# Sparse-attention scores as three single-pass products of split queries and keys instead of one fp32 product

## The reference

```python
qh = q.reshape(...) * (HEAD_DIM ** -0.5)          # 6 heads of 64, in 2 key/value groups of 3
s_s = jnp.einsum('bkgqd,bkqjld->bkgqjl', qi, k_sel).astype(f32) - sl[..., None] * dist[:, :, None]
p_s, _ = _softmax_masked(...)
s_w = jnp.einsum('bkgqd,bknd->bkgqn', qi, kwi).astype(f32) - sl * rel.astype(f32)
p_w, _ = _softmax_masked(s_w, m_w)
o = gi[..., 0:1] * o_c + gi[..., 1:2] * o_s + gi[..., 2:3] * o_w
```

## Time and profile before

| what | value |
|---|---|
| median of 3 runs | 725.65 us (725.53 to 728.75) |
| the profiled execution | 728.8 us |
| its span, first to last instruction | 727.0 us |
| PE busy | 706.1 us (97%) |
| PEld busy | 568.8 us (78%) |
| DVE busy | 450.1 us (62%) |
| ACT busy | 365.3 us (50%) |
| mean granted TensorE clock | 0.992 |

### The profile page before, as it was taken

How to read it: one execution, slowest core, us unless ns; L and a number is a source line. 1 busy time by engine, 2 the same in 40 slices (tenths; PEclk the granted TensorE clock), 3 DMA queues, 4 the chain that set the end, 5 groups by cost and what they waited for, 6 DMA issues and landing times. The chain is left out here.

```text
span 727.0 us, 10208 instructions
## 1 busy us (share of the span) xinstructions
PE 706.1 (97%) x4182; PEld 568.8 (78%) x4182; DVE 450.1 (62%) x647; ACT 365.3 (50%) x565; POOL 11.6 (2%) x20
## 2 busy tenths in 40 slices
PE   5999999999999999999999999999999999999898
PEld 5889888889755566887887888778887888887787
DVE  2677873347655555266369748694659759649544
ACT  6673554565565654347545444443445343264641
POOL 2000000000000000003000000000000000000000
PEclk9999999999999999999999999999999999999899
DMA  9505333320210103731213251134112123313102
GB/s 357 206 36 174 121 138 115 110 91 35 86 60 5 54 2 117 283 151 53 72 50 117 71 218 59 58 116 174 58 59 103 71 87 115 117 59 115 59 14 102
DMA packets 13838, 74.31 MB, mean 102 GB/s; under 512 B 1824, under 2 KB 3904, under 8 KB 6112
## 3 DMA queue, kind: packets, MB, share of 16 engines
q1 hardware_dynamic: 13392, 70.56, 27.1%
q0 software_dynamic: 256, 3.11, 1.0%
q10 hardware_dynamic: 144, 0.00, 0.0%
HBM read 70.51 MB, written 2.10 MB: 100 GB/s over the span
## 5 line engine op out<-in xcount | busy, mean ns | idle before, releaser
L1636 PE MATMUL bank<-Xhi,Whi 128*128 128x512 f32 (+1 forms) x480 | 188.3, 392 | 2.2 <-DVE Wlo L1446 1.0
L1637 PE MATMUL bank<-Xlo,Whi 128*128 128x512 f32 (+1 forms) x480 | 186.2, 388 | 0.0
L1638 PE MATMUL bank<-Xhi,Wlo 128*128 128x512 f32 (+1 forms) x480 | 186.2, 388 | 0.0
L1636 PE MATMUL bank<-Whi,Uhi 128*128 128x512 f32 (+1 forms) x304 | 116.7, 384 | 0.8 <-DVE Wlo L1101 0.5
L1637 PE MATMUL bank<-Wlo,Uhi 128*128 128x512 f32 (+1 forms) x304 | 114.9, 378 | 0.0
L1638 PE MATMUL bank<-Whi,Ulo 128*128 128x512 f32 (+1 forms) x304 | 114.9, 378 | 0.0
L1636 PEld LDWEIGHTS bank<-Xhi,Whi 128*128 128x128 f32 x480 | 90.7, 189 | 26.9 <-issue 6.9
L1638 PEld LDWEIGHTS bank<-Xhi,Wlo 128*128 128x128 f32 x480 | 90.7, 189 | 18.6
L1637 PEld LDWEIGHTS bank<-Xlo,Whi 128*128 128x128 f32 x480 | 90.8, 189 | 17.3
L1101 DVE TENSOR_TENSOR Wlo<-raw,Whi 128x2048 fp32r<-128x2048 f32 x28 | 64.1, 2290 | 48.7 <-ACT Whi L713 48.7
L1110 DVE TENSOR_TENSOR Wlo<-arena,Whi 128x2048 fp32r<-128x2048 f32 x20 | 45.7, 2287 | 51.1 <-ACT Whi L721 51.1
(11 more groups left out here) (230 smaller groups left out, 867.0 us busy)
## 6 DMA issues: line engine op xcount, KB each, us to landing
raw<-wst SPq DMA_DIRECT2D x43, 1024.0 KB, 4.8
arena<-wst SPq DMA_DIRECT2D x16, 1024.0 KB, 4.9
arena<-ctab POOLq DMA_DIRECT2D x1, 2880.0 KB, 9.6
arena<-xn SPq DMA_DIRECT2D x4, 512.0 KB, 5.1
arena<-xn SPq DMA_DIRECT2D x1, 2048.0 KB, 7.6
out<-arena SPq DMA_DIRECT2D x7, 256.0 KB, 2.0
arena<-gpost SPq DMA_DIRECT2D x2, 512.0 KB, 7.2
arena<-arena SPq DMA_DIRECT2D x8, 64.0 KB, 2.0
```

What stands on the lines that cost most here:

```text
L1636: mm(out_ap, w[0], x[0], start=start, stop=False, **kw)
L1637: mm(out_ap, w[0], x[1], start=False, stop=False, **kw)
L1638: return mm(out_ap, w[1], x[0], start=False, stop=stop, **kw)
```

## The change

The scores of the 24 units are made from halves. The queries and keys are split ahead: `PARTS` lists five tiles (KS, Q0, KW, Q0+1, Q0+2) and the slot of `Uhi` and `Ulo` that each goes to. ScalarE makes the high halves (`part_high`) and VectorE the low halves (`part_low`): the first two ahead of unit 0, the others in units 0, 1 and 2. `scores` waits for the halves it reads and issues three products for each k, the two k side by side. Since slots 3 and 4 now hold keys, the recurrence's output is kept in a new place `OH` and split at u=21 and u=24. To make room for `OH`, the transposed weights `PT` are packed as triangles.

```diff
-        PT = view(aX, 8192).rearrange("p (a k j t) -> p a k j t", a=2, k=NKV, j=TT)
+        PTW = 13 * P
+        OH = view(aX + 7168, 1024)
+        def pt_columns(a, k, i):
+            o = aX + (NKV * a + k) * PTW + i * P
+            return view(o, 384 * (i + 1)).rearrange("p (j n) -> p j n", n=384)[:, :, 0:P]
+        def pt_rows(a, k, j):
+            return view(aX + (NKV * a + k) * PTW + 4 * j * P, (TT - j) * P)
...
+        PARTS = ((3, KS), (0, Q0), (4, KW), (1, Q0 + 1), (2, Q0 + 2))
+        PART_AT = {0: 2, 1: 3, 2: 4}
...
+                    def part_high(n):
+                        place, tile = PARTS[n]
+                        nc.scalar.activation(Uhi[:, place, :], T[:, tile, :], ACT.Copy).then_inc(qk_hi, 1)
+                    act.wait_ge(job_done, H_JOB[1] + 1)
+                    act.wait_ge(ct_lo, 1)
+                    part_high(0)
+                    part_high(1)
...
-                        if u == 3:
-                            for j in range(2):
-                                act.wait_ge(oh_done, 1)
-                                nc.scalar.activation(Uhi[:, 3 + j, :], tD[:, j * SEQ:(j + 1) * SEQ],
-                                                     ACT.Copy).then_inc(mix_hi, 1)
+                        if u in PART_AT:
+                            part_high(PART_AT[u])
+                        if u in (21, NU):
+                            j = (21, NU).index(u)
+                            act.wait_ge(oh_done, 1)
+                            act.wait_ge(s_mm, NKV * (20 if j == 0 else NU))
+                            nc.scalar.activation(Uhi[:, 3 + j, :], OH[:, j * SEQ:(j + 1) * SEQ],
+                                                 ACT.Copy).then_inc(mix_hi, 1)
...
+                    def part_low(n):
+                        place, tile = PARTS[n]
+                        dve.wait_ge(qk_hi, n + 1)
+                        V2.tensor_tensor(Ulo[:, place, :], T[:, tile, :], Uhi[:, place, :].bitcast(fp32),
+                                         ALU.subtract).then_inc(qk_lo, 1)
+                    part_low(0)
+                    part_low(1)
...
-                        if u == 4:
-                            hg_lo()
+                        if u in PART_AT:
+                            part_low(PART_AT[u])
+                        if u in (21, NU):
+                            hg_lo((21, NU).index(u))
...
-                        for k in range(NKV):
-                            r = slice(k * HD, (k + 1) * HD)
-                            mm(PB[2 * (u % 2) + k][:, 0:(i + 1) * P], T[r, Q0 + g, i * P:(i + 1) * P],
-                               T[r, (KS, KW)[b], 0:(i + 1) * P], start=True, stop=True).then_inc(s_mm, 1)
+                        pe.wait_ge(qk_lo, max(2 if b == 0 else 3, (2, 4, 5)[g]))
+                        for n, (q, kv) in enumerate(((Uhi, Uhi), (Uhi, Ulo), (Ulo, Uhi))):
+                            for k in range(NKV):
+                                r = slice(k * HD, (k + 1) * HD)
+                                last = mm(PB[2 * (u % 2) + k][:, 0:(i + 1) * P], q[r, g, i * P:(i + 1) * P],
+                                          kv[r, 3 + b, 0:(i + 1) * P], start=(n == 0), stop=(n == 2))
+                                if n == 2:
+                                    last.then_inc(s_mm, 1)
```

More of the change, by code:

```diff
@@ L161, in build @@
         SQ, RS = tA.rearrange("p (j t) -> p j t", j=2), tC.rearrange("p (j t) -> p j t", j=2)
[L163 removed]
+        PTW = 13 * P
+        OH = view(aX + 7168, 1024)
+        assert 2 * NKV * PTW <= 7168
+        def pt_columns(a, k, i):
[3 more added lines that the diff above has]
+            return view(aX + (NKV * a + k) * PTW + 4 * j * P, (TT - j) * P)
         SR = view(aX + 8192, SRD * NKV * SEQ).rearrange("p (a n) -> p a n", a=SRD * NKV)
@@ L301, in build @@
         oh_done = sem("oh_done")
+        qk_hi = sem("qk_hi")
+        qk_lo = sem("qk_lo")
         mix_hi = sem("mix_hi")
@@ L864, in t_copy @@
                             act.wait_ge(t_mm, NKV * u + k + 1)
-                            nc.scalar.activation(PT[:, a, k, 0:i + 1, i * P:(i + 1) * P],
+                            nc.scalar.activation(pt_columns(a, k, i),
                                                  PB[TRB[k]][:, 0:(i + 1) * P].rearrange("p (j t) -> p j t", t=P),
@@ L1304, in hg_out, with hg_lo @@
                         dve.wait_ge(hgo_ev, 2)
[L1305 to L1311, removed]
+                        V2.tensor_tensor(OH, tB, tC, ALU.mult).then_inc(oh_done, 1)
+                    def hg_lo(j):
+                        dve.wait_ge(mix_hi, (2, 4)[j])
+                        V2.tensor_tensor(Ulo[:, 3 + j, :], OH[:, j * SEQ:(j + 1) * SEQ], Uhi[:, 3 + j, :].bitcast(fp32),
+                                         ALU.subtract).then_inc(mix_lo, 1)
+                    def part_low(n):
[5 more added lines that the diff above has]
+                    part_low(1)
                     def cmp_keys():
@@ L1428, in _ @@
                             if grp in (1, 3) and part == TT - 1:
-                                mix_lo_part(grp // 2, 2 + grp // 2 + 1)
+                                mix_lo_part(grp // 2, grp)
                     dve.wait_ge(mix_hi, 6)
@@ L1954, in values @@
                             pe.wait_ge(t_ev, NKV * TT * (grp + 1))
-                            if b == 0:
-                                pe.wait_ge(mix_lo, 2 + g)
+                            if b == 0 and g:
+                                pe.wait_ge(mix_lo, g if g == 1 else 3)
                         for k in range(NKV):
                             last = mm(PB[OB][k * HD:(k + 1) * HD, s * P:SEQ], V[:, (VS, VW)[b], s, k * HD:(k + 1) * HD],
-                                      PT[:, grp % 2, k, s, s * P:SEQ], start=(b == 0 and s == 0), stop=False)
+                                      pt_rows(grp % 2, k, s), start=(b == 0 and s == 0), stop=False)
                         if b == 1 and s == TT - 1:
```

## The result

The changed kernel took **728.89 us** (median of 18 runs, 727.65 to 730.97), the kernel before 725.73 us (18 runs, 722.89 to 728.87). The medians are 3.2 us apart; the ratio is 1.0039, 95% interval 1.0025 to 1.0053, which is 0.4% slower or some 2.8 us. The forecast was 728.1 us and 2.5 us more. The profiled execution of the changed kernel took 730.89 us, with a span of 728.2 us against 727.0 before.

A forecast was written before the change was run, and what follows sets the result against it. TensorE, busy 97% of the span, was taken as the bound. Pause 2.7 plus split 0.5 less 0.7 kept from the scores gave 2.5 us more: 725.65 becomes 728.1 us, range 723.5 to 733.5.

The forecast's parts named there:

- of it lost in waits: Scores blocks ahead of waits set by ScalarE and VectorE: net 0.26 us of the gain disappears into longer waits.
- rival C: The 2.7 us pause ahead of unit 0 makes the clock fall: 1.5 us more, 729.6 us; chance 0.20.
- Step 1: 24 scores blocks: three overlapping pairs of half-type products, fixed 0.21 us kept; 1.0 us less, 0.7 of it kept.
- Step 2: Ahead of unit 0's scores: TensorE idles 2.7 us for one ScalarE copy, then two VectorE subtractions.
- Step 3: Other splits: `part_high(2)` ahead of panel 15's split makes the wait at 162.44 grow by 0.5 us.
- The parts costed at nothing: Parts 3 and 4 in units 1 and 2: late rows of units 2 and 3 are covered, no cost.
- At u=24: Output split: rows of unit 25 start 0.75 us late, at most 0.2 comes through, costed at nothing.
- A: Scores blocks: pairs of half-type products do not overlap, six distances paid; 13.8 us more, 739.5 us; chance 0.10.
- B: Scores blocks: second and third weight loads of the same rows wait for the matmul ahead; 5.3 more, 733.4 us; chance 0.07.
- D: 128-key scores blocks: products cost the upper bound, 0.21 us each; 1.6 more, 729.2 us; chance 0.15.
- E: Scores blocks: the fixed 0.21 us belongs to float32 and vanishes; 5.0 less, about 723.5 us; chance 0.07.

The follow-up runs named there:

- e1: Changed kernel with TensorE's spread matmuls of unit 0, and ScalarE's copies to match, put ahead of unit 0's scores: 724.14 us, ratio 0.9986.
- e2: Kernel before, float32 scores, with the same reordering as e1 (spread of unit 0 ahead of its scores): 725.39 us, ratio 1.0011.
- e7: Changed kernel with a fourth product, low x low, in each of the 24 units: one run, 731.76 us beside 726.02.
- e8: e1 with VectorE's low halves of the later panels moved one unit later, behind that unit's rows and scaling: 720.54 us, ratio 0.9943.
- e9: Kernel before, float32 scores, with both reorderings of e8: 721.37 us, ratio 0.9949.
- e3: Changed kernel with all its splits and waits, but scores again made as one float32 matmul per half: 729.40 us, ratio 1.0059.
- e6: Changed kernel with ten unused 512-column matmuls keeping TensorE busy in the pause ahead of unit 0, scores no earlier: 727.81 us, ratio 1.0029.
- e4: Changed kernel with the loops exchanged, the three products of one k issued first, then the three of the other: 728.85 us, ratio 1.0051.
- e5: Changed kernel with the selected keys (KS) split earlier, so one low half instead of two stands ahead of unit 0: 727.75 us, ratio 1.0035.

## Why the prediction was right

728.1 us was forecast and 728.89 measured, within 0.5% of the kernel before. By its steps:

| term | forecast | measured |
|---|---|---|
| pause ahead of unit 0 | +2.7 | +2.78 |
| split of panel 15 later | +0.5 | +0.52 |
| blocks, all 24 | -1.0 | -1.8 (e1 against e2) |
| of it lost in waits | 0.26 | 0.6 |
| clock | 0 (rival C: +1.5) | +2.8 for one fall, -1.5 for another, in the two profiles |
| stage | +2.5 | +3.43 |

**Step 1** had its mechanism right: fixed part kept, three distances, pairs side by side. 0.89, 0.72 and 0.545 us are the forecast's 0.90, 0.735 and 0.57. The mis-sized term is the 128-key block: I took 0.12 for each distance and left the fixed 0.21 beside it, and got 0.57; it is 0.48. e7 shows why: its inner steps are 0.11, the distance of the weight loads and the lower bound I had, and the first step of 0.16 already holds part of the fixed 0.21. Six such blocks are 0.5 of the 0.8 us by which the gross gain was underrated. **What is lost in waits** grew with the gain, and ends just where it was said to: behind units 2, 7, 11 and 18, by 0.07, 0.21, 0.22 and 0.08. The kept gain is 1.2 (e1 against e2) instead of 0.7. e8 and e9 bear the cause out, since without these waits all of it arrives.

**Step 2** came out to 0.1 us, with its whole chain. **Step 3** too: 0.83 in e3 against 0.31 before. (Half of 1.16 is 0.58, which the forecast put down as 0.5; 0.52 came.) The parts costed at nothing brought no wait between unit 2's and unit 7's. At u=24 the low half ran at 265.65 and the rows of unit 25 began at 267.31, 2.36 later than in the earlier trace rows; some 1.9 of it is the shift of the whole stage, so 0.5 is left of the 0.75 allowed for. A new wait of 0.09 at 256.24 and 0.10 more at 280.81 are all that TensorE shows from unit 21 on.

**The rivals.** A, B, D and E are refuted by the blocks and the loads above: 0.89 us, neither 1.59 nor 0.7, and 0.48 at 128 keys. B was a rule of the Trainium skill, TensorE: Matmul & The Clock Gate, Part 3 (the mechanism), by which a load overlaps matmuls in flight only when its row group differs. The trace disagrees in every block: the load at 213.70 goes to the rows on which the product of 213.59 is running, and the next product starts only at 213.93. The same section also lets a load run ahead when it goes to the background weight buffer, and with that the trace is consistent.

**C came true**, at a chance of 0.20: the forecast itself had the clock at nothing. C had its part as one more fall of 1.5 us. In the profiled execution the fall after the pause took 2.8 (0.68 on the first block, 2.1 on the spread and `cmp_mlp` behind it; e6, without it, is 2.9 shorter), about twice, since it was 6.8 us long; and the old fall after unit 3, worth 1.5, was gone, though the 24 small products stand there as before. The net +1.3, less the 0.5 us more that was kept of the blocks, carries the forecast's 2.5 nearly to the 3.43 of the stage. The old fall is absent from the one profile of all ten other kernels, e2 and e9 with their float32 products among them, and in e2, e6 and e8, at 0.998, the only fall ahead of the span's end stands between 668 and 674 us. The 31 of 46 executions of before at 0.998 have room for one such fall, so most of them probably lack the one in the stage. The prediction read it in an execution that it knew to be 3.1 us above the median, and took it for a trait of the kernel. Why it comes in some executions and not in others stays open.

For the medians this gives a simpler account. Without the clock the change costs 2.78 + 0.52 - 1.2 = 2.1 us, and the executions at 0.998 are 2.2 apart. The median execution went from 0.998 to 0.995, and the medians are 3.2 apart, which leaves 1.1 for the clock. So the forecast was 0.4 too high in what it summed, since it kept too little of the blocks' gain, and lacked 1.1 for the clock. That the two misses have opposite signs is luck, and it brought 728.1 as near to 728.89 as it is; the costs of the pause and of the split are not.

## What to carry to other kernels

A new operand form has two prices, and the second is where it is made: with TensorE busy for 97% of the span, the two copies and two subtractions ahead of the first use cost 2.8 us of idle, and the fall of the clock behind it as much again in the profiled execution (1.1 by the medians), while the cheaper scores gave back 1.2. Put work that doesn't need the new operand there (e1 turned 0.4% slower into 0.1% faster). Then look at which waits lie behind the places that got faster: a third of the gain went into them, and moving the work that ends them (0.4% from e1 to e8, 0.6% from e2 to e9) was worth more than the change itself. And before a fall of the clock is read out of a profile, compare that execution's time and mean clock with the others': here both main profiles had a lower mean clock than their medians.

## What was not expected of the hardware

- The order of two independent 64-row streams in the program hardly matters (0.16 us over 24 blocks): e4 issues three products of one half of the rows and then three of the other, and the trace has the same pairs at the same times to 0.01 us (213.59, 213.93, 214.16). The Trainium skill, TensorEngine Tiling (Array Packing), Key Properties, says that tiles can load and multiply independently of each other; the trace agrees, and shows it for the order of issue too.
- A pair of half-type products costs one distance: 0.23 us at 512 columns, 0.17 at 384, 0.12 at 256, and at 128 the 0.11 of its weight load (e7).
- After the pause of 2.5 us the clock was at 1.2 GHz for 6.8 us in the changed kernel, e3 and e4, but for 3.4 us in e7 at the same pause, and for 3.4 us after the 1.9 us pause of e5. With TensorE busy through the pause it did not fall (e1, e6, one profile each). A price taken from one such fall can be off by a factor of two.
